# Another order of steps from rotations to attention, and the w_o product of two token tiles by parts of the inner dimension

## What is computed

```python
z = x @ w_in + b_in            # q, k, v (768 each), ua, ub (512 each), gate columns (2 x 1024)
q, k = partial_rotary(q), partial_rotary(k)
attn = three groups of dilated window attention, merged     # 256 wide, prompt and cached keys
u = ua * sigmoid(ub); conv = causal_depthwise(u, width 31)  # 512 channels
branch_c = silu(layer_norm(conv)) @ w_conv_out + b_conv_out
branch_a = attn @ w_attn_out
y = (sigmoid(g_a) * branch_a + sigmoid(g_c) * branch_c) @ w_o
h = layer_norm(alpha * x + y)
out = layer_norm(alpha * h + moe(h))   # top 1 of 4 groups, then top 2 of 8 experts in it
```

## Time and profile before

| | us |
|---|---|
| median of 3 runs | 1245.51 (1243.91 to 1245.95) |
| the profiled execution | 1245.54 |
| its span in the trace | 1243.5 |
| PE busy | 1146.5 (92%) |
| DVE busy | 827.3 (67%) |
| ACT busy | 575.2 (46%) |
| POOL busy | 268.1 (22%) |

### The profile page before, as it was taken

How to read it: one execution, slowest core, us unless ns; L and a number is a source line. 1 busy time by engine, 2 the same in 40 slices (tenths; PEclk the granted TensorE clock), 3 DMA queues, 4 the chain that set the end, 5 groups by cost and what they waited for, 6 DMA issues and landing times.

```text
span 1243.5 us, 16070 instructions
## 1 busy us (share of the span) xinstructions
PE 1146.5 (92%) x5990; PEld 908.5 (73%) x5990; DVE 827.3 (67%) x945; ACT 575.2 (46%) x524; POOL 268.1 (22%) x185
## 2 busy tenths in 40 slices
PE   6999999979899999799589999999999999999980
PEld 5999998868688778676457777777777777777760
DVE  1089999500401573633669998888888888889856
ACT  2322211111301236100347877787787778777850
POOL 2344520000000002400112233223322332332110
PEclk9999999989867999898689999999999999999995
DMA  6468632145130064021669999999999999999823
GB/s 250 160 245 310 243 145 82 46 170 188 48 102 34 13 259 140 1 102 71 281 207 358 371 371 368 355 359 348 374 361 352 360 361 361 359 359 376 318 76 145
DMA packets 40336, 293.06 MB, mean 236 GB/s; under 512 B 10927, under 2 KB 14639, under 8 KB 24557
## 3 DMA queue, kind: packets, MB, share of 16 engines
q1 hardware_dynamic: 26029, 262.53, 55.7%
q0 software_dynamic: 10720, 25.98, 7.0%
q10 hardware_dynamic: 3552, 4.06, 1.0%
HBM read 286.83 MB, written 41.12 MB: 264 GB/s over the span
## 4 chain that ended last, share of the span: by engine, by line
PE 86%; DVE 5%; DMA 3%; issue 2%; POOL 2%; ACT 1%; SPq 1%; POOLq 0%; ACTq 0%; DVEq 0%
PE ps L580 9%; PE ps L870 9%; PE ps L872 9%; PE ps L871 9%; PE ps L894 5%; PE ps L896 5%; PE ps L895 5%; PE ps L542 3%; PE ps L544 3%; PE ps L543 3%; PE ps L712 2%; PE ps L788 2%; PE ps L853 2%; PE ps L818 2%; PE ps L820 2%
## 5 line engine op out<-in xcount | busy, mean ns | idle before, releaser
L1549 DVE TENSOR_TENSOR region_b_split<-region_b,z_split 128x2048 fp32r<-128x2048 f32 x96 | 216.9, 2286 | 26.1 <-ACT z_split L1103 25.5
L1549 DVE TENSOR_TENSOR region_a_split<-region_a,z_split 128x2048 fp32r<-128x2048 f32 x96 | 216.7, 2285 | 23.2 <-ACT z_split L1103 23.1
L870 PE MATMUL ps<-z_split,scratch_split 128*96 128x512 f32 x512 | 206.6, 404 | 1.9 <-DVE scratch_split L1554 1.9
L872 PE MATMUL ps<-z_split,scratch_split 128*96 128x512 f32 x512 | 202.0, 395 | 0.0
L1103 ACT CAST z_split<-region_a 128x2048 fp32r<-128x2048 f32 x96 | 179.9, 1909 | 0.0
L1103 ACT CAST z_split<-region_b 128x2048 fp32r<-128x2048 f32 x94 | 176.1, 1908 | 2.0 <-PE ps L872 2.0
L580 PE MATMUL ps<-x_columns,region_b 128*128 128x272 f32 x512 | 142.2, 429 | 9.0 <-DMA region_b<-in_w_in_pairs 9.0
L1242 DVE SCALAR_TENSOR_TENSOR z_conv_gates<-scratch,column_vectors,z_conv_gates 128x512 f32<-128x512 f32 (+1 forms) x240 | 133.9, 630 | 0.0
L580 PEld LDWEIGHTS ps<-x_columns,region_b 128*128 128x128 f32 x512 | 102.5, 207 | 30.1 <-DMA region_b<-in_w_in_pairs 9.1
L542 PE MATMUL ps<-z_split,region_b_split 128*128 128x272 f32 x384 | 111.1, 289 | 3.5 <-POOL region_b_split L1652 3.5
L544 PE MATMUL ps<-z_split,region_b_split 128*128 128x272 f32 x384 | 111.2, 290 | 0.0
(11 more groups left out here) (264 smaller groups left out, 1804.2 us busy)
## 6 DMA issues: line engine op xcount, KB each, us to landing
region_b<-in_w_expert_gate SPq DMA_DIRECT2D x16, 2048.0 KB, 11.9
region_a<-in_w_expert_up SPq DMA_DIRECT2D x16, 2048.0 KB, 11.9
region_a<-in_w_expert_gate SPq DMA_DIRECT2D x16, 2048.0 KB, 11.7
region_a<-in_w_expert_down SPq DMA_DIRECT2D x16, 2048.0 KB, 11.5
region_b<-in_w_expert_up SPq DMA_DIRECT2D x16, 2048.0 KB, 12.4
region_b<-in_w_expert_down SPq DMA_DIRECT2D x16, 2048.0 KB, 11.5
region_b<-in_w_in_pairs SPq DMA_DIRECT2D x21, 1024.0 KB, 4.8
region_b<-in_cache_tiles POOLq DMA_DIRECT2D x16, 768.0 KB, 4.6
```

Of the source, the lines that this page charges most:

```text
L870: pe.matmul(out, xh[:, k, :], hi[:, k, :], start=k == 0, stop=False)
L872: last = pe.matmul(out, xl[:, k, :], hi[:, k, :], start=False, stop=k == KD - 1)
L1549: ve.tensor_tensor(low_part[place][:, part], raw[place][:, part], high_part[high or w][:, part].bitcast(F32), ALU.subtract).then_inc(low_s ...
```

## The change

In the list, quarters are dealt out anew: 8 over the rotations, 3 over the values, none ahead of `sample_rows` and `new_keys`, 2 ahead of the last two `cached_keys`, 1 and 3 ahead of `sample_turn` and `sample_probs`, 2 ahead of each `cached_values`, so that 5 are left for `attend`. The norm of the convolution is cut in five steps (`conv_mean`, `conv_square`, `conv_var`, `conv_root`, `conv_silu`) that stand behind blocks 1, 2, 3, 4 and 6 of `cached_values`. `cen` moves to the scratch buffer. VectorE's `conv_mean` no longer waits for stores; its first `mask_max` waits for Silu; ACT waits for the stores of key rows ahead of the first expert's weights. `store_rows` moves behind the eighth pair load.

The w_o product of tiles 0 and 1 goes by k: for k from 0 to 5 one part for both tiles, once that part of the operands is there, then k = 6 and 7 for each tile. It begins when seven branches have been read. VectorE makes each `ga_lo` two branches behind. Routers 0 and 1 both follow tile 2; `logits_out` comes one tile later, and ACT takes the roots of both first tiles first.

```diff
@@ -200,7 +200,7 @@
-        acc, cen = ua, ub
+        acc, cen = ua, sc[:, 0:CT * N].rearrange("p (c n) -> p c n", c=CT)
         rstd_c = ps[:, 2:4, 0:HALF]
@@ -360,14 +360,19 @@
-        order = [("conv_rows", 0, 12)] + [("rotate", m, 1) for m in range(12)] + [("values", m, int(m < 4)) for m in range(6)]
-        order.append(("sample_rows", 0, 1))
...
+        order = [("conv_rows", 0, 12)] + [("rotate", m, int(m % 3 < 2)) for m in range(12)] + [("values", m, int(m % 2 == 0)) for m in range(6)]
+        order.append(("sample_rows", 0, 0))
         for b in range(NB):
-            order.append(("cached_keys", b, 1))
+            order.append(("cached_keys", b, 1 if b < 6 else 2))
             if b < 6:
                 order.append(("keys", b, 1))
-        order += [(kind, 0, 1) for kind in ("new_keys", "conv_mean", "sample_turn", "conv_var", "sample_probs")]
-        order += [("cached_values", b, 1) for b in range(NB)]
+        order += [("new_keys", 0, 0), ("sample_turn", 0, 1), ("sample_probs", 0, 3)]
+        norm = {1: "conv_mean", 2: "conv_square", 3: "conv_var", 4: "conv_root", 6: "conv_silu"}
+        for b in range(NB):
+            order.append(("cached_values", b, 2))
+            if b in norm:
+                order.append((norm[b], 0, 0))
         spare = 4 * 16 - sum(step[2] for step in order)
@@ -437,8 +442,7 @@
                 load_pair(13 + g, G0 // 2 + g)
-                if g == 3:
-                    store_rows()
+            store_rows()
@@ -771,7 +775,8 @@
                     gate_quarter(q)
-                work[kind](i)
+                if kind in work:
+                    work[kind](i)
@@ -790,12 +795,10 @@
-            pe.wait_ge(w_split, SPLIT + 4)
-            pe.wait_ge(x_split, 2 + KD)
-            pe.wait_ge(wr_loaded, 32)
...
                 c0, n = TILES[t]
+                if t == 0:
+                    pe.wait_ge(wr_loaded, 32)
                 pe.wait_ge(hdone, t + 1)
@@ -809,18 +812,35 @@
-            for t, (c0, n) in enumerate(TILES):
-                if t >= 2:
-                    pe.wait_ge(y_used, t - 1)
+            def rows_out(t, ks):
...
+                c0, n = TILES[t]
                 for half in range(2):
                     out, cols = ps[0:n, 2 * (t % 2) + half, :], slice(half * 512, (half + 1) * 512)
-                    for k in range(KD):
+                    for k in ks:
                         pe.matmul(out, ga_hi[:, k, c0:c0 + n], wo_hi[:, k, cols], start=k == 0, stop=False)
...
                         last = pe.matmul(out, ga_lo[:, k, c0:c0 + n], wo_hi[:, k, cols], start=False, stop=k == KD - 1)
-                last.then_inc(y_ps, 1)
-                if t >= 1:
-                    router(t - 1)
+                return last
...
+            pe.wait_ge(br_used, KD - 1)
+            for k in range(KD - 2):
+                if k % 2 == 0:
+                    pe.wait_ge(w_split, SPLIT + k // 2 + 1)
+                pe.wait_ge(x_split, 2 + k + 1)
+                for t in range(2):
+                    rows_out(t, [k])
+            pe.wait_ge(w_split, SPLIT + 4)
+            pe.wait_ge(x_split, 2 + KD)
+            for t in range(2):
+                rows_out(t, range(KD - 2, KD)).then_inc(y_ps, 1)
+            for t in range(2, NTT):
+                pe.wait_ge(y_used, t - 1)
+                rows_out(t, range(KD)).then_inc(y_ps, 1)
+                if t == 2:
+                    router(0)
+                router(t - 1)
             router(NTT - 1)
@@ -1036,13 +1056,15 @@
-            def conv_mean(_):
+            def conv_square(_):
                 ac.wait_ge(cen_sb, 2 * CT + 1)
...
-            def conv_var(_):
+            def conv_root(_):
                 ac.wait_ge(veps, 1)
...
+            def conv_silu(_):
                 ac.wait_ge(cnorm, 1)
@@ -1060,7 +1082,7 @@
             work = dict(conv_rows=conv_rows, sample_rows=sample_rows, keys=key_rows,
-                        sample_turn=sample_turn, conv_mean=conv_mean, conv_var=conv_var, attend=attend)
+                        sample_turn=sample_turn, conv_square=conv_square, conv_root=conv_root, conv_silu=conv_silu, attend=attend)
             for kind, i, quarters in steps:
@@ -1087,10 +1109,17 @@
-            for t, (c0, n) in enumerate(TILES):
-                s = t % 2
+            def root(t):
+                n = TILES[t][1]
                 ac.wait_ge(hvar, t + 1)
-                ac.activation(sd[s][0:n], var_e[s][0:n], ACT.Sqrt).then_inc(hsd, 1)
+                ac.activation(sd[t % 2][0:n], var_e[t % 2][0:n], ACT.Sqrt).then_inc(hsd, 1)
...
+            root(0)
+            root(1)
+            columns_out(0)
+            columns_out(1)
+            for t in range(2, NTT):
+                root(t)
                 columns_out(t)
@@ -1103,6 +1132,8 @@
             ac.wait_ge(y_ps, NTT)
+            for s in range(2):
+                ac.wait_ge(krow_stored[s], 16 * 3)
             for w in "gu":
@@ -1298,9 +1329,7 @@
                 ve.wait_ge(mean_ps, 1)
-                ve.wait_ge(stored, 16 * STORES)
-                for s in range(2):
-                    ve.wait_ge(krow_stored[s], 16 * 3)
+                ve.wait_ge(u_ps, 1)
@@ -1323,6 +1354,8 @@
                 ve.wait_ge(qk_ps, i + 1)
+                if i == 0:
+                    ve.wait_ge(cact, CT)
                 if i >= 2:
@@ -1361,11 +1394,15 @@
                         sample_turn=sample_turn, sample_probs=sample_probs, cached_values=cached_values,
-                        conv_mean=conv_mean, conv_var=conv_var, attend=attend)
+                        conv_mean=conv_mean, conv_var=conv_var, conv_root=conv_root, attend=attend)
             for kind, i, _ in steps:
...
+            def merged_low(m):
+                ve.wait_ge(x_high, 2 + m + 1)
+                ve.tensor_tensor(ga_lo[:, m, :], ga[:, m, :], ga_hi[:, m, :].bitcast(F32), ALU.subtract).then_inc(x_split, 1)
@@ -1379,10 +1416,10 @@
-            for m in range(KD):
-                ve.wait_ge(x_high, 2 + m + 1)
-                ve.tensor_tensor(ga_lo[:, m, :], ga[:, m, :], ga_hi[:, m, :].bitcast(F32), ALU.subtract).then_inc(x_split, 1)
+                if m >= 2:
+                    merged_low(m - 2)
+            merged_low(KD - 2)
+            merged_low(KD - 1)
@@ -1398,6 +1435,12 @@
+            def logits_out(t):
+                n = TILES[t][1]
+                ve.wait_ge(lg_ps, t + 1)
+                ve.tensor_tensor(lg[0:n, t, :], ps[0:n, 6 + t % 2, 0:36], br[0:n], ALU.add).then_inc(lg_sb, 1)
@@ -1414,12 +1457,10 @@
                 ve.scalar_tensor_tensor(hs, hs, rs[s][0:n], b1row[0:n], ALU.mult, ALU.add).then_inc(hdone, 1)
-                if t >= 1:
-                    c1, n1 = TILES[t - 1]
-                    ve.wait_ge(lg_ps, t)
-                    ve.tensor_tensor(lg[0:n1, t - 1, :], ps[0:n1, 6 + (t - 1) % 2, 0:36], br[0:n1], ALU.add).then_inc(lg_sb, 1)
-            ve.wait_ge(lg_ps, NTT)
-            ve.tensor_tensor(lg[0:NS, 4, :], ps[0:NS, 6, 0:36], br[0:NS], ALU.add).then_inc(lg_sb, 1)
+                if t >= 2:
+                    logits_out(t - 2)
+            logits_out(NTT - 2)
+            logits_out(NTT - 1)
             ve.wait_ge(lg_sb, NTT)
```

## The result

| | before | after |
|---|---|---|
| median of the runs, us | 1245.73 (1243.91 to 1246.73) | 1209.43 (1205.38 to 1210.14) |
| profiled execution, us | 1245.54 | 1205.38 |
| its span, us | 1243.5 | 1203.4 |
| PE busy, us | 1146.5 | 1124.9 |

The changed kernel takes 0.9703 of the time before, with a 95% interval of 0.9679 to 0.9728: 36.3 us off, where 46 were forecast. The profiled execution is 4 us under the median; this difference turns out to be part of the answer.

A forecast was written before the change was run, and what follows sets the result against it. PE was taken to bound the kernel, losing clock and waiting between rotations and router; 35.6 (order up to attention) + 10.3 (w_o product) = 45.9 off 1245.5 gave 1199.6, say 1199.5, range 1193 to 1215 us.

The forecast's parts named there:

- the first (the clock holds only partly): Rival, cached values: first quarter after each block runs at 1.2 GHz, 12 us lost, 1211.5 us; chance 0.15.
- third rival: Rival, w_o product: taking it by parts gains nothing, only the order changes, + 8 to 10 us, 1208.5; chance 0.09.
- The cached values at 1.00: Cached-values blocks: with two quarters each PE's clock rises from 0.61 to 1.00, removing 23.5 us.
- two thin spots: New-keys products and 12 extra products ahead of block 0: clock falls of 0 to 1.7 us each, charged 2.0 together.
- part 1: Order of PE's work from rotations to attention, quarters dealt out anew: 35.6 us off in sum.
- The stores: Input-weight pair load: row stores moved behind the eighth pair load remove PE's wait and slow clock, 10.6 us.
- The norm: Convolution norm: spreading its steps between cached-values blocks removes 5.6 us of PE idle time.
- new wait for Silu: Ahead of attention: VectorE's first mask_max waits for ScalarE's Silu; cost nothing, at worst 0.5 us.
- New stalls: Added PE waits: 2.6 us more at rotations and values (3.0 in all), 1.1 at sample_rows, 0.5 in attention.
- Attention without quarters: Attention: three more heads without a quarter cost PE 0.5 us more, at most 3.
- Part 2: w_o product by parts: idle time, slow first tiles and one router clock fall go, 10.3 us off in sum.
- a longer fall behind the pair of routers: Routers 0 and 1 run together after tile 2: longer clock fall, 0.5 us charged, up to 2 more possible.

The follow-up runs named there:

- the stores experiment: Kernel before with only the 20 stores of rows moved from behind the fourth to behind the fifth load of a gate pair: 1237.3 us, ratio 0.9922.
- part 2 alone: Kernel before with only the w_o product of two tiles by parts, low parts in the branch loop, routers 0 and 1 behind tile 2: 1234.0 us, ratio 0.9901.
- after again: The changed kernel run once more without any edit, on the chip of later runs: 1209.8 us, ratio 0.9701 to the kernel before.
- norm in one place: Changed kernel with the convolution norm's steps back together ahead of the cached values, blocks keeping two quarters: 1215.0 us, ratio 0.9757 to the kernel before.

## Why the prediction was right, and where its sizes were off

- **Way and bound.** Right: PE bounds the kernel, the loss lay in clock more than in waits, and nothing came back in the expert loop. Of the rivals none happened as told; the nearest is the first (the clock holds only partly). 1211.5 was its time, 1209.4 the measured one, but its picture, a slow quarter behind each block, is not the trace's: most blocks are followed by none and some by a whole one.
- **The range.** The forecast's own range was 1195 to 1207, and 1209.4 lies above it. It lies within 1193 to 1215 only because the range was drawn out to the first and third rival. The central forecast was 9.9 us too fast, mainly by one term that it had priced too low, and the width of the range covered that. Over the cached values the clock was 0.92 in the profiled execution; under 0.9 was to be a sign of being wrong, and the second profiled execution had 0.90. The margin was thin.
- **The cached values at 1.00** is the term that was mis-sized. The step took the row of the cached keys, 1.00 from 271.7 to 307.8, as the price of this mixture, and charged 2.0 for two thin spots. Measured were four stretches of low clock, 8.5 us, in the profiled execution and 13.6 in another. The 6.5 beyond the 2.0 charged account for the 6.3 that part 1 fell short. Of the two thin spots the new keys lost nothing in the first execution, and the 12 extra products with block 0 lost 3.4, twice the full price of 1.7 that was put on it. The 4 us between the profiled execution and the median go with the mean clock (0.963 against 0.959 to 0.960); in which stretch they lie is not shown, since the median execution has no trace. The row of before was a lucky one: with the same blocks the stores experiment lost 3.4 near there.
- **The stores:** 10.6 as one term; alone 7.9. The wait went whole; falls behind it took some back.
- **The norm:** 5.6; undone from the kernel after, 5.5 by the medians. The new wait for Silu never showed.
- **New stalls:** forecast 3.0 at the values and 1.1 at the sample rows, 4.1 in all; measured 1.5 + 1.4 + 0.9 = 3.8. VectorE's pace set the end as said; 1.4 of the 2.9 at rotations and values were lost at the third rotation already. Attention without quarters: PE stood 1.4 us from 401.0 to 440.7, against 1.3, so the 0.5 was not needed.
- **Part 2:** 10.3; 11.2 between the profiles of before and after, and 11.2 alone by the medians. The agreement is in part luck: in three further profiles with the pair of routers, the pair left a longer fall. From the end of the branches to tile 4's last w_o product they take 72.4 us (part 2 alone), 73.5 (after again) and 73.6 (norm in one place), against 70.9, so the gain there is 8.5 to 9.7. The first w_o product follows the last branch product at once, and GpSimd's add was 3.32 us beside VectorE where 4.1 was the bound, so the shared interface that the Trainium skill names (GPSIMD Engine Reference, section 1 Specifications) cost the branches nothing: they take the same 44 us. In the kernel after:

```profile
482.43 3.32 POOL L1722 TENSOR_TENSOR z_conv_gates<-z_conv_gates 128x544 f32<-128x544 f32 x1 [2.03 <-DVE z_conv_gates L1412]
484.47 1.86 DVE L1405 TENSOR_TENSOR z_split<-z_conv_gates,z_split 128x544 fp32r<-128x544 f32 x1
485.25 1.08 PE L795 MATMUL ps<-attn_columns,w_attn 128*128 128x272 f32 x4
...
485.97 0.60 PE L821 MATMUL ps<-region_a_split,z_split 128*128 128x512 f32 x1
```

  VectorE's low part itself took 1.86 us beside GpSimd in place of 0.79, and still fitted in 5.5.
- **The clock.** The prediction put 0.5 on a longer fall behind the pair of routers, and up to 2 more by the rule that it took from the Trainium skill (TensorE: Matmul & The Clock Gate, Part 4). In the first profiled execution the stage came out 0.9 better than the sum; in the three others it was 1.5 to 2.7 us longer than there. So 2 us were about the right size and 0.5 was too little, though no run shows that the transposes are the reason. Part 1 of the same page of the Trainium skill speaks of idle time before a fall. In this case the clock also fell with PE busy throughout (60.3 us at 0.61), so a busy share read from a profile does not tell whether the clock holds.

What stays open: why the same program falls behind one block in one execution and behind another in the next. Nor is it shown whether the routers lose the clock by their narrow work or by the 1.1 us for which PE stands in them.

## What to carry to other kernels

Read PEclk beside PE's busy share stretch by stretch: a stretch that is 100% busy at 0.61 hides more time than all waits around it. Where narrow products and wide ones share PE, deal them out finely: the same products cut in runs half as long kept the clock in most executions, which gained 11 us in the blocks. The same cut in the routers gained 10, of which 3.3 were waits. And take the clock of a stretch from several executions before it carries a forecast.

## What the runs showed of the hardware

- The clock falls from 2.4 to 1.2 GHz without any idle time of PE, behind runs of narrow products (2.58 us at full clock; 60.3 us at a granted 0.61 in the kernel before). It also falls behind routers (transposes, 1.1 us in which PE stands, and 36-column sums, 4.0 us in all). With the runs halved it stayed at 1.00 from 245 to 368 us in three profiled executions, and in a fourth, with two quarters more ahead of thin spots, it was at 0.68 for 16 us.
- Falls are not reproducible in place: over the same instructions they cost 8.5 us in one execution and 13.6 in another, behind the routers 3.1 and 6.2, and run times from 1205.2 to 1213.5 follow the mean clock, 0.963 to 0.957.
